# Reordering the first loads of a fused transformer kernel: x ahead of the modulation weights, the first projection by quarters

## What is computed

```python
mod = silu(c) @ w_mod + b_mod          # 6 x 1024 columns; mod_c likewise from c_ctx
sh1, sc1, gt1, sh2, sc2, gt2 = split(mod, 6)
h  = rms_norm(x, g_pre1) * (1 + sc1) + sh1       # rms_norm: over the 1024 features of a token
hc = rms_norm(ctx, g_pre1) * (1 + sc1c) + sh1c   # ctx: 256 tokens of 1024 features
qn, kn, vn, qh, zf, zb, ih, gh = split_cols(h @ w_in)   # w_in: 1024 x 4096
...                                               # the same of hc, for the context
```

## Time and profile before

| | us |
|---|---|
| median of three runs (lowest, highest) | 2674.57 (2674.56, 2683.15) |
| profiled execution, span from the first to the last instruction | 2689.2 |
| PE busy in it | 2163.9 (80%) |
| DVE, ACT, POOL busy | 599.4, 343.5, 97.0 |
| moved by DMA | 755.20 MB, mean 281 GB/s |

### The profile page before, as it was taken

The page is one execution under the profiler, slowest core; times in us unless marked ns, Lnnn a source line. Parts: engine busy times, 40 slices in busy tenths (PEclk is TensorE's granted clock), DMA queues, the critical chain, the costliest instruction groups (busy, mean ns, idle before and its releaser), DMA issues.

```text
span 2689.2 us, 35584 instructions
## 1 busy us (share of the span) xinstructions
PE 2163.9 (80%) x15740; PEld 1251.1 (47%) x15740; DVE 599.4 (22%) x1143; ACT 343.5 (13%) x692; POOL 97.0 (4%) x116
## 2 busy tenths in 40 slices
PE   5999998555566565666988865587999999999999
PEld 2444574222223232233554432263576885666874
DVE  1112554001011010112322210055434000461000
ACT  2101222000010000011110100031251000132000
POOL 0001000000000000000111100000030000100000
PEclk8999998999999999999999999988899999999999
DMA  8633706999999999999999999953732454323450
GB/s 329 260 127 140 236 10 230 421 425 425 424 424 422 421 425 415 421 407 424 424 424 424 425 424 425 421 185 105 240 127 63 139 178 153 110 79 113 148 204 37
DMA packets 158907, 755.20 MB, mean 281 GB/s; under 512 B 12249, under 2 KB 75737, under 8 KB 102050
## 3 DMA queue, kind: packets, MB, share of 16 engines
q1 hardware_dynamic: 158754, 752.92, 70.6%
HBM read 751.83 MB, written 1.05 MB: 280 GB/s over the span
## 4 chain that ended last, share of the span: by engine, by line
PE 54%; DMA 40%; DVE 3%; ACT 2%; issue 1%; POOL 0%; DVEq 0%; SPq 0%; ACTq 0%; POOLq 0%
DMA ring<-w_up_dram 16%; PE psum L653 11%; DMA ring<-w_gate_dram 11%; DMA ring<-w_down_dram 8%; PE psum L555 8%; PE psum L681 5%; DMA ring<-hyb_w_dram 4%; PE psum L1176 3%; PE psum L467 2%; PE psum L1560 2%; PE psum L1240 2%; PE psum L446 2%; PE psum L1284 2%; PE psum L1382 1%; PE psum L1655 1%; PE psum L1015 1%
## 5 line engine op out<-in xcount | busy, mean ns | idle before, releaser
L1176 PE MATMUL psum<-ring,arena 128*32 128x320 f32 x4096 | 360.4, 469 | 281.0 <-DMA ring<-w_gate_dram 141.9
L1176 PEld LDWEIGHTS psum<-ring,arena 128*32 128x32 f32 x4096 | 112.0, 111 | 440.6 <-DMA ring<-w_up_dram 170.8
L653 PE MATMUL psum<-arena,ring 128*128 128x256 f32 x1408 | 305.5, 380 | 0.0
L1240 PE MATMUL psum<-ring,arena 128*32 128x512 f32 x1344 | 212.0, 606 | 107.3 <-DMA ring<-w_down_dram 107.3
L653 PEld LDWEIGHTS psum<-arena,ring 128*128 128x128 f32 x1408 | 268.5, 191 | 36.6
L555 PE MATMUL psum<-ring,arena 128*128 128x512 f32 x480 | 213.3, 606 | 10.3 <-ACT arena L2760 8.5
L1240 PEld LDWEIGHTS psum<-ring,arena 128*32 128x32 f32 x1344 | 47.4, 109 | 247.2 <-DMA ring<-w_down_dram 171.8
L555 PEld LDWEIGHTS psum<-ring,arena 128*128 128x128 f32 x480 | 92.7, 195 | 128.2 <-issue 128.2
L2337 DVE TENSOR_TENSOR arena<-arena,psum 128x320 f32<-128x320 f32 (+1 forms) x32 | 16.7, 521 | 580.5 <-PE psum L1176 574.6
L681 PE MATMUL psum<-ring,arena 128*128 128x512 f32 x288 | 125.0, 596 | 0.0
L1185 PE MATMUL psum<-ring,arena 128*32 128x64 f32 x2048 | 119.8, 291 | 0.0
(11 more groups left out here) (376 smaller groups left out, 2121.0 us busy)
## 6 DMA issues: line engine op xcount, KB each, us to landing
ring<-w_gate_dram SPq DMA_DIRECT2D x128, 1376.0 KB, 18.1
ring<-w_up_dram SPq DMA_DIRECT2D x128, 1376.0 KB, 18.1
ring<-w_down_dram SPq DMA_DIRECT2D x112, 1536.0 KB, 19.9
ring<-w_mod_dram SPq DMA_DIRECT2D x72, 1024.0 KB, 5.1
ring<-w_ffn_in_dram SPq DMA_DIRECT2D x88, 512.0 KB, 5.1
ring<-w_ffn_out_dram SPq DMA_DIRECT2D x14, 1536.0 KB, 7.4
ring<-w_in_dram SPq DMA_DIRECT2D x16, 1024.0 KB, 5.6
ring<-hyb_w_dram SPq DMA_DIRECT2D x10, 1024.0 KB, 16.8
```

The source lines that it names most:

```text
L653: ins = nc.tensor.matmul(b[:, i * 256:(i + 1) * 256], ws[k // 4][:, k % 4, u, i * P:(i + 1) * P], R(XT + k * 256, 256), start=(k == 0), st ...
L1176: ins = nc.tensor.matmul(banks[u][c][32 * j:32 * j + 32, 0:GMAIN], R(XST + k * HALF + e * CAP, CAP), w3[:, 64 * c:64 * c + 64, QGROUP * j: ...
L1240: ins = nc.tensor.matmul(ybanks[half][32 * c:32 * c + 32, :], stationary, w, start=((half, c) not in begun), stop=(unit >= 36), skip_group ...
```

## The change

SP now loads x directly behind the column constants, then two blocks of `w_mod`, the identity alone with a semaphore of its own (`ident_loaded`), the modulation bias and the other six blocks. ctx stands behind the first column block of `w_in`, the row constants behind the first four blocks of the second modulation group, the rest of the matrix constants behind the next four, and the post gains four blocks later still.

PE waits for the identity ahead of the seventh part of the first group, and makes the 16 transposes of x there. The wait for all banks of x is gone: `project` has a parameter `arriving`, with which each quarter of the first projection (a half of the features, a tile of tokens) waits for its own bank. The wait for `consts` stands after the fourth projection.

DVE waits for x, normalises it, and waits for `cols` only then; its wait for `rows` stands behind the context's normalising, and that for `consts` ahead of the first rotary embedding. ACT no longer waits for `rows`.

```diff
-            def project(tag, key, tiles, n, ctx_first=None):
+            def project(tag, key, tiles, n, arriving=None):
...
                     for t in tiles:
+                        if arriving:
+                            pe.wait_ge(bank_drained[bank_of((arriving, t, h))], nth((arriving, t, h)))
                         for k in range(4):
...
             for k in range(KT):
+                if k == KT - 2:
+                    pe.wait_ge(ident_loaded, 16 * tally.due(ident_loaded))
+                    normalised_T("x1", XN)
                 modulation_part("mod1", 0, k, 6, "c1")
-            pe.wait_ge(consts_loaded, 16 * tally.due(consts_loaded))
-            normalised_T("x1", XN)
             modulation_cols("mod1", 0)
-            transposed("x1")
             for n, c in enumerate(IN1_BLOCKS):
-                project("in1", c, range(4) if c in (1, 2, 4, 5, 6) else range(2), HALF)
+                project("in1", c, range(4) if c in (1, 2, 4, 5, 6) else range(2), HALF, "x1" if n == 0 else None)
+                if n == 3:
+                    pe.wait_ge(consts_loaded, 16 * tally.due(consts_loaded))
...
-            v.wait_ge(consts_loaded, 16 * tally.due(consts_loaded))
-            v.wait_ge(cols_loaded, 16 * tally.due(cols_loaded))
-            v.wait_ge(rows_loaded, 16 * tally.due(rows_loaded))
             v.wait_ge(x_loaded, 16 * tally.due(x_loaded))
             normalise(X, XN)
+            v.wait_ge(cols_loaded, 16 * tally.due(cols_loaded))
...
             normalise(R(CX, 2048).rearrange("p (t n) -> p t n", t=TT), CX)
+            v.wait_ge(rows_loaded, 16 * tally.due(rows_loaded))
...
+                if c == 0:
+                    v.wait_ge(consts_loaded, 16 * tally.due(consts_loaded))
...
-            a.wait_ge(rows_loaded, 16 * tally.due(rows_loaded))
             a.wait_ge(x_loaded, 16 * tally.due(x_loaded))
...
             load(cols[:, :], T["cols"], cols_loaded)
-
-            mod_in("mod1", T["w_mod"], 0, 0, 3)
-            load(consts[:, :], T["consts"], consts_loaded)
             rows_in(x[:, :], T["x"], x_loaded)
-            mod_in("mod1", T["w_mod"], 0, 3, 6)
+            mod_in("mod1", T["w_mod"], 0, 0, 2)
+            load(const("ident"), T["consts"][:, 0:P], ident_loaded)
             biases(T["b_mod"], MB)
-            mod_in("mod1", T["w_mod"], 0, 6, KT)
-            load(rows[:, :], T["rows"].partition_broadcast(P), rows_loaded)
-            rows_in(R(CX, 2048), T["ctx"], ctx_loaded)
+            mod_in("mod1", T["w_mod"], 0, 2, KT)
             for n, c in enumerate(IN1_BLOCKS):
                 proj_in("in1", T["w_in"], c * 512, 512, c)
+                if n == 0:
+                    rows_in(R(CX, 2048), T["ctx"], ctx_loaded)
                 if n < 4:
                     mod_in("mod1", T["w_mod"], 1 + n // 2, 4 * (n % 2), 4 * (n % 2) + 4)
                 if n == 0:
+                    load(rows[:, :], T["rows"].partition_broadcast(P), rows_loaded)
+                elif n == 1:
+                    load(consts[:, P:], T["consts"][:, P:], consts_loaded)
+                elif n == 2:
                     post_rows(T["g_post1"], T["g_post2"])
```

More of the change, by code:

```diff
@@ L155, in program @@
         consts_loaded = semaphore("consts_loaded")
+        ident_loaded = semaphore("ident_loaded")
         normed_ready = semaphore("normed_ready")
```

## The result

Twelve runs of the changed kernel have a median of 2666.53 us (2659.24 to 2677.8), twelve of the kernel before, taken beside them, 2686.02 (2670.14 to 2696.42). The ratio is 0.9938 with a 95% interval of 0.9917 to 0.9959: 16.7 us faster, 11 to 22. The forecast was 14.3 us. Both intervals reach across half a per cent, so on which side of that line the gain lies is not settled.

The account below looks back on a forecast made before the run. The front was taken as bound by transfers until 31.7, then by a serial chain over three engines to 48.25. First projection at 34.0 instead of 48.25 saves 14.3 us: 2674.57 - 14.3 = 2660.3 us, range 2655 to 2670.

Parts of the forecast that it names:

- Step 1: Front's loads: all constants but the identity leave from ahead of the last weight block; last modulation part can begin at 28.1.
- Step 2: x loaded ahead, there at 7.1, normalised under the modulation's loads by near 13; without that cover it costs 5.7 us.
- Step 3: End of first modulation group: 16 transposes ahead of the seventh part, last part ending at 29.6 (29.0 to 31).
- Step 4: From modulation's end to first projection: exchange between PE and DVE, waits by quarter, 4.4 us; projection begins at 34.0.
- Step 5: First projection at the lower clock: the same loss as before, 2.4 us, give or take 0.9.
- Rival B: Clock stays up across the shorter idle ahead of the first projection: gain 16.7 us, 2657.9; chance 0.08.
- Step 6: Loads moved behind the front (ctx, row constants, other constants, post gains) arrive in time: cost 0.
- The sum: First projection at 34.0 instead of 48.25, all later work shifted alike: 14.3 us gained, median 2660.3.
- Rival C: Gain lost later to transfers in the experts' stretch, a third left: 2670; chance 0.06.
- rival D: Slower: rest of the constants on SP's queue, between second modulation group and block 4, at 50 GB/s: 2681.9; chance 0.04.
- Rival A: Clock comes up late, in the last modulation parts or first projection: gain 12.3 us, 2662.3; chance 0.20.

Follow-up runs that it names:

- the second comparison: The changed kernel, unaltered, timed once more against the kernel before on the same chip: ratio 0.9950 (0.9923 to 0.9976), 13.4 us faster.
- the two delayed versions: Changed kernel with six extra 1024 KB blocks loaded ahead of everything, once or in three rounds; ratios to the kernel before 0.9962 and 1.0094.
- the two that go on from the changed kernel: Changed kernel plus 27 idle transposes, ratio to the kernel before 0.9908; on top, smaller first load, copy-by-copy waits, idle transposes rearranged (10 and 26), 0.9892.

## Why the prediction was right

- **Step 1, transfers.** Forecast: last part possible at 28.1. Measured: its block was there by 27.83, when PE's weight load of the last part ends its wait, or by 28.12 and 28.13 in two other traces where the part itself waits; putting 1506.5 KB back moved the last part to 31.74. Right.
- **Step 2, x ahead.** Squares at 7.04 (7.1), done at 12.77 (13). Right, and without its cover the work costs 5.0 to 7.6 us, where 5.7 was said.
- **Step 3, end of the modulation.** 29.06 against 29.6, inside 29.0 to 31. The text had the clock at its lower level until 27 to 28. In fact it had come up during the fourth part (1.54 us, then 1.07 for the fifth), was down again for the sixth (1.94) after waits of 0.94 and 1.41 us (granted 0.82 in the stretch from 21.5 to 22.8, 0.50 from there to 24.7), and rose once more within the 16 transposes, which took 2.44 us where 3.4 was said. The end gained little by it, since the last block was not there before about 27.8.
- **Step 4, to the projection.** 29.06 to 33.22 is 4.16 against 4.4. All the quarters but the first were free, as said: the chain shows the 32 records without a break. What the text did not see: by the program the first quarter's wait is there twice, since the bank's reuse asks for the same.
- **Step 5, the clock.** The loss in the first projection is 17.04 - 13.93 = 3.1 us in one trace and 15.37 - 13.93 = 1.4 in another; 2.4 give or take 0.9 was said, which the second misses by 0.1. Rival B, the clock staying up across the shorter idle, happened in none of the seven traces with the changed kernel's waits by quarter and no idle transposes in the gap. The run with idle transposes shows that it was priced rightly.
- **Step 6, what moved behind.** Nothing was late for PE. The row constants landed at 48.3 (47.4 was said). DVE stood 8.63 us for the row constants and drained the first bank at 49.03, with nobody behind it.
- **The sum.** The first projection came 15.0 us earlier, 0.8 more than said; the slower projection took 0.7 of it back, and 14.1 us were left at the start of the attention in one trace and 14.4 in the other, against 14.3; 16.7 and 13.4 us measured. The step that the text took from structure alone, that the shift passes through the experts' stream, is shown by the table: 1304 to 1306 us everywhere. Rival C falls with it, rival D with the absence of any wait for a DMA. Rival A falls too: the last part ended at 29.1, and the first projection ran 0.7 us longer than before at most.

The mechanism is right, step by step. That the whole time also agrees to 1 and 2.4 us is in part luck: the intervals are 11 and 14 us wide, and at equal clock the second comparison leaves 10.3 us.

The span forecast for the profiled execution, 2674.9, was wrong by 17.4 us. The sum against one execution's span left out that two executions of one kernel differ by more than the change is worth (2657.5 and 2668.9 for the changed kernel). The text allowed 3 us for the clock's later ups and downs; the second and fourth stages scatter by 14 and 11.

**Open.** Why the two delayed versions and the two that go on from the changed kernel meet a higher clock (0.972 to 0.973 in the mean, where the kernel before has 0.965 to 0.966). The table at equal clock shows that their 8 to 11 us beyond the front go with that clock, not what sets it. The higher clock is seen with the changed kernel's order of the front (0.968 to 0.973) and hardly with the old one (0.966 and 0.967); no run here settles whether the order brings it, and part of the 16.7 us is of that kind.

## What to carry to other kernels

Cut the trace where the bound changes, and compare stage by stage, with the busy times of the engines that the change does not touch as a check: here that separated 14.1 us of gain from 16.6 of clock in a single pair of traces, and every experiment on a front of 50 us could be read to 1 to 3 us from one trace, where the whole time scatters by 20. Where versions differ by less than the scatter, set the mean granted clock of the runs beside their times: groups that meet different clocks do not compare by time alone. When work is drawn ahead under a stream of loads, look at what PE does at the end of that stream, and at the wait for a reused bank, before shrinking the loads or splitting the wait further. Where PE must idle ahead of a dense stretch, instructions that compute nothing can be cheaper than the lower clock they prevent; here that is shown for the stretch behind them (1.4 to 3.1 us), not for the whole time.

## What was unexpected of the hardware

- The granted clock is no guide before its first change in a trace. The kernel before reads 1.00 from 7 to 36.0 us (the end of it in the earlier trace rows), yet seven parts in it took 1.94 us each, while four parts took 3.64 later, 0.91 each, close to the ratio of 1.2 to 2.4 GHz. The durations tell.
- The same instructions on the same data take 172.8 to 186.9 us between attention and experts, with the clock alone at work.
- 27 transposes of no use, laid where PE was idle, took 1.4 to 3.1 us off the projection behind them: the clock can be held up in this way.
- Gaps of 0.94 and 1.41 us around one part at full rate were enough to bring the clock down in the changed kernel: granted 0.50 behind them, and the next part took 1.94 us again. Its second trace (0.89 and 1.43 us) shows the same.
